# Attention over all keys by pairs of heads, with the row sums of the weights taken on GpSimd

## The chip, the cores and the metric

The kernel runs on one core of one Trainium2 chip. The metric is the device time of one execution in microseconds (us), the median of several runs. The engines are named as in the profile: PE (TensorE, matmuls), PEld (its weight loads), DVE (VectorE), ACT (ScalarE), POOL (GpSimd), SP (SyncE, which only issues DMAs).

## The reference

Two transformer blocks follow each other on 1024 tokens of width 1024, in float32. The change lies in the first block's attention: 8 query heads of width 64, heads 0 to 3 on one key and value head, heads 4 to 7 on the other, every query sees every key.

```
    def one_block(q_blk):
        s = jnp.einsum('bkgqd,bksd->bkgqs', q_blk, kt).astype(jnp.float32) * scale
        p = jax.nn.softmax(s, axis=-1).astype(vt.dtype)
        return jnp.einsum('bkgqs,bksd->bkgqd', p, vt)
```

Around it stand an input projection (23 tiles of 128 columns), a bidirectional mLSTM with 4 heads, an output projection and a gated feed-forward part. The second block has its own projections, an attention with forget gates and one over a sliding window.

## The kernel before

The kernel is written by hand for one core. A planner (`Plan`) first writes one list of steps; each engine then walks through the list and issues its own instructions for the steps that concern it, in that order, and semaphores hold the engines together. So the list sets the order on every engine, and an instruction that waits holds up all that stands behind it on its engine.

The full attention goes by jobs (kind, head h, half n of the queries: 512 columns), 16 in all, one after the other, h outermost. A job has 8 units, one for each 128 keys. All is kept transposed: keys on partitions, queries along the free dimension. For a unit:

- `sc`: PE makes 128x512 scores in one of two PSUM banks (2 and 3) with two matmuls, `qq,kk` and `qa,ka`; the second adds the low parts and, by a row of ones, minus the row maximum. ACT then takes the exponential into one of three buffers `full_pf`.
- `val`: PE multiplies these weights by the values. The stationary tile `full_v` is 128 keys x 128 columns: 64 columns of values and 64 of ones, so rows 64 to 127 of the result are the row sums. Both operands are float32; the profile shows each such product as two records. Banks 6 and 7 alternate by job.
- `max`: for a later job, PE makes scores once more with queries on partitions, and DVE takes the maximum of each row (8 of these per job, one per unit); `mrow` turns the 4x128 maxima into a row, which ACT writes into `full_qa`. `max`, `mrow` and some steps of the mLSTM's gates alternate between two further banks, 4 and 5.
- `take` and `div`: ACT turns the row sums into their inverse (Ln, then Exp with scale -1), DVE multiplies the 64x512 result by it.
- `qhi`, `qlo`: ACT and DVE split the queries of a later job into high and low parts, three buffers.

In `attention`, the step `sc` of the next unit stands ahead of `val` of this one. Between them `other(...)` takes portions of the input projection from a list (`fill`: nine matmuls each, L1218 to L1220), as long as there are any, and hooks place steps of the mLSTM there: its gates ("gate") beside units 3 to 63, the preparation of its first head beside the last 26 units. After the last job the first mLSTM outputs (L1456) wait until all 16 divisions are done.

Lines to follow: L1309 (`max` on PE), L1325 (`mrow` on PE), L1344 and L1346 (`sc`), L1368 (`val`), L1831 (exponential), L1839 and L1841 (`take`), L1811 (`mrow` on ACT), L2292 (maximum on DVE), L2156 and L2160 (DVE products and low parts).

## Time and profile before

| | us |
|---|---|
| median of 3 runs | 1990.89 |
| lowest and highest | 1988.49, 1994.8 |
| the profiled execution, device time | 1993.19 |
| its span in the trace | 1991.4 |
| the full attention's stretch of the trace | 279 to 520 |

How to read it: the span runs from the first to the last instruction; the device time of the same execution is 1.8 us more. Time in the trace is counted from the start of the span. Busy time of PE is summed over records that overlap, since a matmul's record runs from its start until its last result is written, while the next one has already begun; the distance from start to start, or the chain of work, tells what a matmul costs.

### The profile page before, as it was taken

The page shows a single profiled execution, that of the slowest core. Times are in us where ns is not written, and L with a number is a line of the kernel's source. Part 1 is how long each engine was busy: PE and PEld are TensorE (multiplying, and loading weights), DVE is VectorE, ACT ScalarE, POOL GpSimd, SP SyncE. Part 2 cuts the span into 40 slices and gives each one's busy share as a digit, 9 for nine tenths or more (in the row PEclk, how much of TensorE's full clock was granted, in tenths as well). Part 3 has the DMA queues.
Part 4 walks back from the last instruction along what each step waited for, and adds up shares of the span by engine and source line. Part 5 has one row for each costly group of instructions (what it writes and reads, how often), then busy time and mean ns, then how long its engine had stood idle before and what let it go on. Part 6 is the DMA issues. An engine that isn't in the chain of part 4 may idle for free.

```text
span 1991.4 us, 23686 instructions
## 1 busy us (share of the span) xinstructions
PE 1929.0 (97%) x8844; PEld 1507.2 (76%) x8844; DVE 1209.3 (61%) x1774; ACT 909.6 (46%) x1523; POOL 104.3 (5%) x188
## 2 busy tenths in 40 slices
PE   6999999999999989999999999999999999999898
PEld 4778876656787768888888788887888887776577
DVE  7795847655576787677555546656453555345744
ACT  6543345565553542332333434434523665455652
POOL 1101100000000000111000100000011000000000
PEclk9999999999999999999999999999999999999999
DMA  8426510010204423345111653333432000114052
GB/s 329 158 96 212 189 33 11 1 53 1 96 1 164 164 96 122 142 180 201 69 70 53 216 207 122 112 128 137 163 132 74 33 32 33 31 39 165 1 180 95
DMA packets 67151, 216.13 MB, mean 109 GB/s; under 512 B 8272, under 2 KB 13520, under 8 KB 66784
## 3 DMA queue, kind: packets, MB, share of 16 engines
q1 hardware_dynamic: 47168, 141.15, 20.1%
q0 software_dynamic: 19872, 73.48, 10.2%
q8 instruction: 72, 1.18, 0.2%
q14 instruction: 39, 0.32, 0.0%
HBM read 177.30 MB, written 34.61 MB: 106 GB/s over the span
## 4 chain that ended last, share of the span: by engine, by line
PE 85%; DVE 7%; ACT 3%; DMA 3%; issue 2%; SPq 0%; DVEq 0%; ACTq 0%
PE ps L1218 13%; PE ps L1220 13%; PE ps L1219 13%; PE ps L1368 9%; PE ps L1524 6%; PE ps L1525 6%; PE ps L1526 6%; PE ps L1344 3%; PE ps L1346 3%; DMA w_raw<-in_weights 2%; PE ps L1309 1%; DVE w_lo L2160 1%; PE ps L1312 1%; ACT w_hi L1691 1%; DMA ada_first<-in_ada 1%
## 5 line engine op out<-in xcount | busy, mean ns | idle before, releaser
L1218 PE MATMUL ps<-h_hi,w_hi 128*128 128x512 f32 x832 | 334.7, 402 | 9.7 <-DVE h_lo L2160 6.5
L1220 PE MATMUL ps<-h_hi,w_lo 128*128 128x512 f32 x832 | 325.9, 392 | 0.0
L1219 PE MATMUL ps<-h_lo,w_hi 128*128 128x512 f32 x832 | 325.4, 391 | 0.0
L2160 DVE TENSOR_TENSOR w_lo<-w_raw,w_hi 128x1024 fp32r<-128x1024 f32 x139 | 170.0, 1224 | 237.3 <-ACT w_hi L1691 235.7
L1691 ACT ACTIVATE w_hi<-w_raw 128x1024 fp32r<-128x1024 f32 x140 | 147.7, 1056 | 239.0 <-DMA w_raw<-in_weights 238.8
L2292 DVE TENSOR_REDUCE mh<-ps 128x1 f32<-128x512 f32 (+1 forms) x224 | 140.2, 630 | 143.9 <-PE ps L1309 67.9
L1218 PEld LDWEIGHTS ps<-h_hi,w_hi 128*128 128x128 f32 x832 | 157.9, 190 | 45.1 <-DVE h_lo L2160 7.7
L1220 PEld LDWEIGHTS ps<-h_hi,w_lo 128*128 128x128 f32 x832 | 156.9, 189 | 34.0
L1219 PEld LDWEIGHTS ps<-h_lo,w_hi 128*128 128x128 f32 x832 | 157.4, 189 | 32.1 <-issue 1.4
L1218 PE MATMUL ps<-hid_hi,w_hi 128*128 128x512 f32 x352 | 138.1, 392 | 3.9 <-DVE hid_kept_lo L2160 2.1
L1524 PE MATMUL ps<-t_hi,pair_S_r 128*128 128x512 f32 x352 | 137.2, 390 | 4.4 <-DVE pair_S_r L2160 2.6
L1220 PE MATMUL ps<-hid_hi,w_lo 128*128 128x512 f32 x352 | 137.0, 389 | 0.0
L1525 PE MATMUL ps<-t_lo,pair_S_r 128*128 128x512 f32 x352 | 137.0, 389 | 0.0
L1526 PE MATMUL ps<-t_hi,pair_S_r 128*128 128x512 f32 x352 | 136.9, 389 | 0.0
L1368 PE MATMUL ps<-full_pf,full_v 128*128 128x512 f32 x256 | 131.0, 593 | 0.3 <-ACT full_pf L1831 0.2
L1831 ACT ACTIVATE second_pf<-ps 128x512 f32<-128x512 f32 (+2 forms) x128 | 65.1, 510 | 139.9 <-PE ps L1350 61.3
L1831 ACT ACTIVATE full_pf<-ps 128x512 f32<-128x512 f32 x128 | 76.2, 597 | 97.9 <-PE ps L1346 97.4
L1368 PE MATMUL ps<-second_pf,second_v 128*128 128x128 f32 (+3 forms) x336 | 113.4, 439 | 0.8 <-ACT second_pf L1831 0.7
L1344 PE MATMUL ps<-full_qq,full_kk 128*128 128x512 f32 x128 | 90.2, 705 | 0.2 <-issue 0.2
L1344 PE MATMUL ps<-second_qq,second_kk 128*128 128x128 f32 (+3 forms) x168 | 84.3, 502 | 1.7 <-ACT second_pf L1831 0.7
L1218 PEld LDWEIGHTS ps<-hid_hi,w_hi 128*128 128x128 f32 x352 | 66.1, 188 | 20.3 <-DVE hid_kept_lo L2160 2.9
L1524 PEld LDWEIGHTS ps<-t_hi,pair_S_r 128*128 128x128 f32 x352 | 66.1, 188 | 19.3 <-issue 4.0
(405 smaller groups left out, 3842.0 us busy)
## 6 DMA issues: line engine op xcount, KB each, us to landing
w_raw<-in_weights SPq DMA_DIRECT2D x140, 512.0 KB, 3.5
ada_next<-in_ada POOLq DMA_DIRECT2D x32, 512.0 KB, 4.7
ada_last<-in_ada POOLq DMA_DIRECT2D x24, 512.0 KB, 5.1
pair_gate<-in_weights SPq DMA_DIRECT2D x22, 512.0 KB, 3.5
pair_up<-in_weights SPq DMA_DIRECT2D x22, 512.0 KB, 4.5
ada_first<-in_ada SPq DMA_DIRECT2D x8, 1024.0 KB, 17.7
m_scratch<-y POOLq DMA_DIRECT2D x12, 512.0 KB, 5.9
hid_scratch<-hid_out POOLq DMA_DIRECT2D x22, 256.0 KB, 2.3
```

The source lines that it names most:

```text
L1218: e.matmul(o, w_hi[slot][:, tile_of(kw)], hi, start=start, stop=False, skip_group_check=skip)
L1219: e.matmul(o, w_hi[slot][:, tile_of(kw)], lo, start=False, stop=False, skip_group_check=skip)
L1220: return e.matmul(o, w_lo[slot][:, tile_of(kw)], hi, start=False, stop=stop, skip_group_check=skip)
L1344: e.matmul(o, A.kk[kb][:, keys], A.qq[b][:, q], start=True, stop=False, skip_group_check=True)
L1368: x = e.matmul(o, A.v[kb][:, kt, :], A.pf[p3][:, c:c + q1 - q0], start=(u == 0 and kind != "band"), stop=False, skip_group_check=True)
L1524: e.matmul(ps[:, bank, :], a_hi[:, tile_of(k)], b_hi[:, first + k, :], start=start and k == 0, stop=False, skip_group_check=True)
L1525: e.matmul(ps[:, bank, :], a_hi[:, tile_of(k)], b_lo[:, first + k, :], start=False, stop=False, skip_group_check=True)
L1526: x = e.matmul(ps[:, bank, :], a_lo[:, tile_of(k)], b_hi[:, first + k, :], start=False, stop=k == 3, skip_group_check=True)
L1691: return e.activation(dst, src, ACT.Copy)
L1831: e.activation(A.pf[p3][:, c0:c1], ps[:, bank, c0:c1], ACT.Exp, scale=SC).then_inc(s["p_exp"], 1)
L2160: return e.tensor_tensor(dst, src, hi.bitcast(F32), ALU.subtract)
L2292: x = e.tensor_reduce(A.mh[b][:, half, i:i + 1], ps[:, bank, 0:k1 - k0], AX_X, ALU.max)
```

## The change

The order of the full attention's work and the form of its value product are changed; the second block's attention is not.

- Jobs are paired: heads 2m and 2m+1 with the same n. Units of the two alternate (`paired` takes the place of `attention` for this part).
- The value product has only the 64 columns of values as its stationary tile (64 instead of 128 columns). The even head writes PSUM rows 0 to 63 of a bank, the odd head rows 64 to 127 of the same bank. In the built program the two have tiles of 128x64 at column 0 and at column 64 of the array; all other large matmuls have 128x128. Products are issued in groups of four (V_GROUP), which alternate between the two halves.
- The row sums come from elsewhere: GpSimd adds the weights of the 8 units of each head (`psum`, 7 additions of 128x512 per job, 112 in all), and two matmuls per pair against 64 columns of ones (`dsum`) sum them over partitions into the auxiliary banks.
- `take` and `div` are done once for each pair on 128 partitions: 8 instead of 16.
- There are six weight buffers instead of three, four query buffers instead of three.
- All 16 maxima of a pair stand beside units 1 to 12 of the pair before it; the last four units of each pair have none.
- GpSimd's queue also gets one instruction that reloads its library ahead of the first addition.
- Some semaphores are merged; the columns of ones are no longer written into `full_v`.

```diff
+V_GROUP = 4
+def paired(p, jobs, fill, share, at):
...
+    for m, start in enumerate(starts):
+        a, b = jobs[2 * m], jobs[2 * m + 1]
+        steps = [("max", *job, u) for job in (a, b) for u in max_units_of(*job)]
+        low, high = (starts[m - 1] + 1, start - 4) if m else (-4 - len(steps), -4)
+        at_g = [low + n * (high - low + 1) // len(steps) for n in range(len(steps))]
+        for g, step in zip(at_g, steps):
+            maxima.setdefault(g, []).append(step)
+        rows.setdefault(at_g[len(steps) // 2 - 1] + 2, []).append(("mrow", *a))
+        rows.setdefault(start - 2, []).append(("mrow", *b))
...
+    for g, (i, u) in enumerate(units):
...
+        if g + 1 < len(units):
+            p.add("sc", *jobs[units[g + 1][0]], units[g + 1][1])
+        for step in rows.get(g, []) + waiting + queries.get(g, []) + maxima.get(g, []):
+            p.add(*step)
+        waiting = [("div", *x[1:]) for x in waiting if x[0] == "take"]
+        if u:
+            p.add("psum", *job, u)
+        if g and g % V_GROUP == 0:
+            products(units[g - V_GROUP:g])
+        if i % 2 and g == last[i]:
+            ended.append((g + 3, job))
+        if ended and ended[0][0] == g:
+            p.add("dsum", *ended[0][1])
+            waiting.append(("take", *ended.pop(0)[1]))
+        other(share(job))
...
-                self.v = [v_area[i](f"{n}_v{i}", [P, KT, P], F32) for i in range(2)]
+                self.v = [v_area[i](f"{n}_v{i}", [P, KT, 64 if n == "full" else P], F32) for i in range(2)]
...
+                if kind == "full":
+                    e.matmul(ps[rows_of(h), bank, :], A.v[kb][:, u, :], weights[:, :], start=u == 0, stop=u == KT - 1,
+                             skip_group_check=True).then_inc(s["val"], 1)
+                    return
...
+            def weight_sums(kind, h, n):
+                bank, sums = aux_bank("dsum", kind, h, n), A1.sums[take_no(kind, h, n) % 2]
+                aux_free(("dsum", kind, h, n))
+                e.wait_ge(s["p_sum"], no("psum", kind, h, n, KT - 1))
+                for odd in range(2):
+                    x = e.matmul(ps[rows_of(odd), bank, :], ones[:, 0:64], sums[odd][:, :], start=True, stop=True, skip_group_check=True)
+                x.then_inc(s["den_mm"], 1)
...
-                if i > 3:
-                    e.wait_ge(s["val"], i - 3)
+                if i > back:
+                    e.wait_ge(s["val"], i - back)
+                    if kind == "full":
+                        e.wait_ge(s["p_sum"], summed(i - back))
...
+                if kind == "full":
+                    e.wait_ge(s["val"], no("val", kind, h, n, KT - 1))
+                    tt(y[:, QA + h // 2, half_of(n)], ps[:, 6 + job % 2, :], A1.rinv[0][:, :], ALU.mult).then_inc(s["div"], 1)
+                    return
...
+            def weight_sum(kind, h, n, u):
+                pair, i = take_no(kind, h, n), no("sc", kind, h, n, u)
+                total = A1.sums[pair % 2][h % 2][:, :]
+                e.wait_ge(s["p_exp"], i)
+                if u == 1:
+                    if pair >= 2:
+                        e.wait_ge(s["den_mm"], pair - 1)
+                else:
+                    e.wait_ge(s["p_sum"], no("psum", kind, h, n, u - 1))
+                e.tensor_tensor(total, weights_at(kind, i - 2)[:, :] if u == 1 else total, weights_at(kind, i)[:, :], ALU.add).then_inc(s["p_sum"], 1)
```

PE's order in the middle of the full attention, past the input projection, before the change (names: `full_qq2` is the query buffer, `full_kk1` the second key head, `full_pf0` to `full_pf2` the weight buffers):

```order
L1344 MATMUL ps<-full_qq2_141,full_kk1_136 128x512
L1346 MATMUL ps<-full_qa2_144,full_ka1_138 128x512
L1309 MATMUL ps<-full_kk1_136,full_qq0_139 128x512
L1368 MATMUL ps<-full_pf1_148,full_v1_146 128x512
L1344 MATMUL ps<-full_qq2_141,full_kk1_136 128x512
L1346 MATMUL ps<-full_qa2_144,full_ka1_138 128x512
L1309 MATMUL ps<-full_kk1_136,full_qq0_139 128x512
L1368 MATMUL ps<-full_pf2_149,full_v1_146 128x512
```

The same place after the change, around the border of two pairs (L1462 and L1464 are `sc`, L1427 is `max`, L1443 `mrow`, L1485 `val`, L1499 `dsum`):

```order
L1443 MATMUL ps<-ident_r_84,mx1_1_154 1x128 x4
L1462 MATMUL ps<-full_qq0_139,full_kk1_136 128x512
L1464 MATMUL ps<-full_qa0_142,full_ka1_138 128x512
L1462 MATMUL ps<-full_qq1_140,full_kk1_136 128x512
L1464 MATMUL ps<-full_qa1_143,full_ka1_138 128x512
L1485 MATMUL ps<-full_pf0_147,full_v0_145 64x512
L1485 MATMUL ps<-full_pf1_148,full_v0_145 64x512
L1485 MATMUL ps<-full_pf2_149,full_v0_145 64x512
L1485 MATMUL ps<-full_pf3_150,full_v0_145 64x512
```

And the rows a few places further down, with the sums of the pair that has ended:

```order
L1427 MATMUL ps<-full_kk1_136,full_qq2_141 128x512
L1499 MATMUL ps<-p_sums10_166,ones_81 64x512
L1499 MATMUL ps<-p_sums11_167,ones_81 64x512
L1462 MATMUL ps<-full_qq0_139,full_kk1_136 128x512
L1464 MATMUL ps<-full_qa0_142,full_ka1_138 128x512
L1427 MATMUL ps<-full_kk1_136,full_qq2_141 128x512
```

One value product stood between any two units' scores; now four stand together, and between the groups scores of four units follow each other. Even and odd weight buffers belong to the even and the odd head.

At the end of the attention PE had, before:

```order
L1368 MATMUL ps<-full_pf0_147,full_v1_146 128x512
L1368 MATMUL ps<-full_pf1_148,full_v1_146 128x512
L1407 MATMUL ps<-ident_80,y_124 128x128 x8
L1456 MATMUL ps<-m_v0_207,m_w0_198 128x129 x2
```

and has now (L1537 and L1586 are the former L1407 and L1456):

```order
L1485 MATMUL ps<-full_pf4_151,full_v1_146 64x512
L1485 MATMUL ps<-full_pf5_152,full_v1_146 64x512
L1485 MATMUL ps<-full_pf0_147,full_v1_146 64x512
L1485 MATMUL ps<-full_pf1_148,full_v1_146 64x512
L1499 MATMUL ps<-p_sums10_166,ones_81 64x512
L1499 MATMUL ps<-p_sums11_167,ones_81 64x512
L1537 MATMUL ps<-ident_80,y_124 128x128 x8
L1586 MATMUL ps<-m_v0_207,m_w0_198 128x129 x2
```

The last two matmuls of `dsum` stand ahead of the transposes L1537 and wait for GpSimd's last addition.

## Rows read from the trace of the kernel before

**Rows 1.** The page: engines over the whole span.

```profile
PE 1929.0 (97%) x8844; PEld 1507.2 (76%) x8844; DVE 1209.3 (61%) x1774; ACT 909.6 (46%) x1523; POOL 104.3 (5%) x188
```

**Rows 2.** Busy time by stretch: us, then each engine's busy us (instructions), clock, DMA.

```profile
279.00:520.00 241.00, 237.91 (x901) 147.31 (x900) 143.37 (x227) 131.80 (x227) 0.00 (x0) 1.00 0.04 14
```

**Rows 3.** Waits from 279 to 520: us in total, times, longest.

```profile
ACT full_pf L1831 <- PE ps L1346: 97.4, 99, 3.0
DVE mh L2292 <- PE ps L1309: 63.7, 66, 3.1
...
PEld ps L1344 <- ACT full_pf L1831: 8.1, 14, 0.8
```

**Rows 4.** The chain of work, 366.4 to 371: start, us, what.

```profile
368.44 0.23 PE ps L1220
368.67 0.86 PE ps L1368 x2
369.53 0.23 PE ps L1344
369.76 0.23 PE ps L1346
370.00 0.23 PE ps L1309
```

**Rows 5.** Instruction groups, 275 to 521: busy us, mean ns; idle before.

```profile
L1368 PE MATMUL ps<-full_pf,full_v 128*128 128x512 f32 x256 | 131.0, 593 | 0.3 <-ACT full_pf L1831 0.2
...
L1346 PE MATMUL ps<-full_qa,full_ka 65*128 65x512 f32 x128 | 50.7, 396 | 0.0
L1309 PE MATMUL ps<-full_kk,full_qq 128*128 128x512 f32 x120 | 48.4, 403 | 0.0
L1220 PE MATMUL ps<-h_hi,w_lo 128*128 128x512 f32 x30 | 11.8, 393 | 0.0
...
L1325 PE MATMUL ps<-ident_r,mx 128*1 128x128 f32 x64 | 6.5, 223 | 3.6 <-issue 2.4 <-DVE mh L2292 1.0
...
L1831 ACT ACTIVATE full_pf<-ps 128x512 f32<-128x512 f32 x128 | 76.2, 597 | 97.9 <-PE ps L1346 97.4
L1841 ACT ACTIVATE rinv<-rinv 64x512 f32<-64x512 f32 x16 | 10.1, 631 | 0.5
L1839 ACT ACTIVATE rinv<-ps 64x512 f32<-64x512 f32 x16 | 9.5, 593 | 1.6 <-PE ps L1368 1.2
L1811 ACT ACTIVATE full_qa<-ps 1x512 fp32r<-1x512 f32 x16 | 9.3, 584 | 5.7 <-PE ps L1325 5.4
L1691 ACT ACTIVATE full_qq<-y 64x512 fp32r<-64x512 f32 x13 | 8.1, 622 | 0.2
...
L2292 DVE TENSOR_REDUCE mh<-ps 128x1 f32<-128x512 f32 x120 | 82.2, 687 | 66.3 <-PE ps L1309 65.7
```

**Rows 6.** PE's instructions in order of time around one `mrow`: start, us.

```profile
353.94 0.39 PE L1346 MATMUL ps<-full_qa,full_ka 65*128 65x512 f32 x1
354.46 0.40 PE L1325 MATMUL ps<-ident_r,mx 128*1 128x128 f32 x4
354.70 0.47 PE L1309 MATMUL ps<-full_kk,full_qq 128*128 128x512 f32 x1
355.02 0.39 PE L1218 MATMUL ps<-h_hi,w_hi 128*128 128x512 f32 x1
```

**Rows 7.** GpSimd's compute groups over the whole span.

```profile
L2745 POOL CAST band_low<-cmask 128x128 bf16<-128x128 f32 x2 | 2.0, 1016 | 0.0
...
L2753 POOL MEMSET second_v<- 128x512 f32 x2 | 1.1, 531 | 0.1
...
L3107 POOL MEMSET const-float32-1.0<- 128x1 f32 x1 | 0.1, 103 | 0.0
```

**Rows 8.** All engines in order of time at the attention's end.

```profile
518.55 0.60 ACT L1831 ACTIVATE full_pf<-ps 128x512 f32<-128x512 f32 x1 [0.73 <-PE ps L1346]
...
522.39 0.38 PE L1456 MATMUL ps<-m_v,m_w 128*128 128x129 f32 x1 [1.19 <-DVE y L2156]
```

More of the change, by code:

```diff
@@ L832, in build @@
         area = Area(156.25, 174)
[L833 to L837 removed]
+        A1 = Buffers("full", four(64, 72, 80, 88), four(68, 136), area, (76, 92, 144, 94, 146, 78))
+        A1.mx = [area(f"mx1_{i}", [P, 4], F32R) for i in range(4)]
+        A1.mh = [area(f"mh1_{i}", [P, 2, 4], F32) for i in range(4)]
+        area = Area(112, 116)
+        A1.qq.append(area("full_qq3", [P, HT], F32R))
+        A1.qa.append(area("full_qa3", [P, HT], F32R))
+        A1.rinv = [Area(148, 150)("rinv1", [P, HT], F32)] * 2
+        A1.sums = [[Area(start, start + 2)(f"p_sums{i}{odd}", [P, HT], F32) for odd, start in enumerate(starts)]
+                   for i, starts in enumerate(((138, 150), (116, 118)))]
         A2 = Buffers("second", four(104, 108, 112, 116), four(132, 136), Area(120, 132), (148, 152, 156))
@@ L1029, in build @@
         G_COLS = {12: 1, 13: 2, 14: 3, 18: 4}
-        AUX = [x for x in plan.steps if x[0] in ("vprep", "max", "mrow") or x[0] == "gate" and x[1] in G_COLS]
+        AUX = [x for x in plan.steps if x[0] in ("vprep", "max", "mrow", "dsum") or x[0] == "gate" and x[1] in G_COLS]
         AUX_NO = {x: i for i, x in enumerate(AUX)}
@@ L1445, in m_outputs @@
                 if i == 0:
-                    e.wait_ge(s["div"], 16)
+                    e.wait_ge(s["div"], FULL_TAKES)
                 elif d:
@@ L2914, in back @@
                 e.wait_ge(s["val"], no("val", "full", last, 1, KT - 1))
+                if part:
+                    e.wait_ge(s["p_sum"], no("psum", "full", last, 1, KT - 1))
                 e.wait_ge(s["m_kept"], 16 * len(KEPT_ORDER))
```

208 lines of the change are left out of this document (139 added, 69 removed).

## The prediction

> **What bounds the kernel now.** I read the page first: PE is busy 97% of the span, the next engine, DVE, 61% [rows 1]. Then the busy time by stretch: in the full attention, 279 to 520, PE has 237.9 of 241 us, ACT 131.8, DVE 143.4 and GpSimd nothing, at full clock [rows 2]. Then the waits: the large ones are those of ACT and DVE for PE (97.4 and 63.7 us); PE's own wait for an exponential is 8.1 us [rows 3]. So PE is the bound and the others have slack. The change touches this stretch only: from the first memory outputs on, PE's order is the old one. What counts is PE's issue time in these 241 us, and how much of ACT's and DVE's slack it eats.
>
> The chain of work gives prices from start to start: 0.23 us for one matmul of 512 columns, 0.86 for a value product in its two records, so 0.43 a record [rows 4]. With the counts of the groups [rows 5]: 256 score matmuls x 0.23 = 58.9; 120 maxima x 0.23 = 27.6; 128 value products x 0.86 = 110.1; 88 matmuls of the input projection x 0.23 = 20.2; the 16 `mrow` of four short matmuls some 5; the gates and the preparation of the memory some 13 (my estimate from the number of their instructions). That is 235; the remaining 6 are PE's waits today.
>
> **The value products (removed 110, added 69).** The 64 new columns do not shorten a product by themselves: `mrow` loads one column and still pays for its moving columns (four of 128 in 0.24 us, against 0.23 for one of 512) [rows 6]. A gain comes only if products of the two halves of the array run at once. No row of this trace shows two tiles side by side, so I bound it: nothing overlaps (0.86 each), or all does (0.43 for each of the two, half). I take a value between, from the order: the two records of one product use the same half and follow each other, so at strictly ordered starts only the second record of one product can run with the first record of the next, in the other half. Four alternating products are then 5 steps of 0.43 = 2.15 us instead of 3.44. 32 groups x 1.29 = 41.3 us less. The full overlap would be 4 steps, 1.72 us, 55.0 less.
>
> The Trainium skill (TensorE: Matmul & The Clock Gate, Part 3) says that three column tiles measured 2.38 times as fast. Spread evenly this is an efficiency of 0.79 a tile, an estimate of 1.59 for two, and 3.44 / 1.59 = 2.17 us; its twofold bound gives the 1.72. No run here shows it yet.
>
> **The sums on PE (added).** Two products per pair against ones: 3 steps of 0.43 = 1.29, x 8 = 10.3 us (6.9 with full overlap, 13.8 with none).
>
> **Change of tile width (added).** 32 groups and 8 sums, 40 visits to the narrow tiles. `mrow` is such a visit today: its four matmuls start 354.46, the next at 354.70, but the one after at 355.02, 0.32 instead of 0.23 later [rows 4, 6]. 0.09 a visit, 3.6 us.
>
> **Sum of PE's issue time: -41.3 + 10.3 + 3.6 = -27.4 us.** (-44.5 with full overlap.)
>
> **Stalls that come back.** Before, the value product between two scores gave ACT 1.55 us for an exponential of 0.60 [rows 4, 5]. Now four units of scores stand together. With two banks, the scores i+2 start when exponential i has ended; they need 0.63 until written (0.23 + 0.40) and some 0.1 for two signals, the exponential 0.60: 1.35 us for two units, 0.675 each. PE's work is 0.46 a unit, 0.69 with one maximum. So units with a maximum just fit, and units without wait.
> - The last four units of each pair have no maxima: 4 x 0.675 = 2.7 of ACT's pace, and one `mrow` (0.58) and one `qhi` (0.62) stand in ACT's queue there, 3.9 us, against 1.84 of scores and 0.3 of `mrow` on PE: 1.8 us of waiting.
> - Behind `dsum` PE has more maxima, and the second needs the bank that ACT's Ln empties. On ACT the Ln stands behind an exponential whose scores come after `dsum`: Ln ends some 1.86 us behind `dsum`, PE is there after 1.15: 0.7 us. Whoever waits is PE, with scores and products queued behind.
> - DVE in the first four units of a pair has six maxima (4.1 us [rows 5]), a low part, a copy and a division, some 5.9, against 4.5 + 2.15 on PE: it fits behind the products.
>
> 2.5 us x 8 pairs = 20, less the 6 that today's stretch already has: +14. Eight portions of the projection (2.05 us each) still give ACT time in the early pairs, the gates' long operations on ACT and DVE take it back; I let them cancel.
>
> **GpSimd (added, off the path).** 112 additions of 128x512. Nothing like it is in the trace. The same shape written without reading takes 0.53 us, 0.10 of it fixed; a cast of 128x128 takes 1.02, four times that is 4.06 [rows 7]. If a read costs what the write costs (0.43), an addition takes 0.96 to 1.4; I take 1.2. A pair then costs GpSimd 14 x 1.2 = 16.8 us. It has some 28.7 (the stretch that I forecast, 229.6, by 8), and 24 where no projection is left (16 x 0.46 + 16 x 0.23 + 4 x 2.15 + 1.29 + 0.7 for `mrow` and visits = 21.6, and 2.5 of stalls). Six buffers let it lag by some three units. The cover is gone at 1.7 us an addition in the late pairs, at 2.05 in all. The fixed cost of its library comes while it is idle.
>
> The Trainium skill (GPSIMD Engine Reference, 3.1) has 4497 ns for an addition of 2048 float32, an estimate of 1.12 us for 512; by it this work stays hidden.
>
> **ACT, DVE, copies.** 8 pairs of Ln and Exp less (0.59 + 0.63 [rows 5]), 8 divisions less, `full_v` without ones: all on engines that wait for PE, worth nothing by themselves. The additional buffers add no instruction.
>
> **The end.** Before, from the last exponential's start (518.55) to the first memory output it is 3.84 us [rows 8]: product, Ln, Exp, division. Now four products (2.15 instead of 0.86) and `dsum` (1.29) stand there, and the last additions end some 2.7 us behind the exponential, so they are no later than the products. About 2 us more.
>
> **Sum.** -27.4 + 14 + 2 = -11.4 us. The profiled execution took 1993.2 (span 1991.4 and 1.8 around it), which gives 1981.8; it lies 2.3 above the median of the runs, so 1979.5, and I say 1979.
>
> **Rivals.**
> 1. Full overlap of the halves, the second record of one head with that of the other: -44.5 + 14 + 2 = -28.5, 1962. For it: nothing in the rows forbids it. Against it: the order of starts. It is also where ACT would bind sooner, so 1962 is near the best. Chance 0.14.
> 2. The overlap is there, but waits eat it: each narrow visit drains PE, and the four units in a row run at ACT's pace everywhere. A drain is a record's 0.39 less the 0.23 = 0.16 us on the way in and again on the way out, 40 x 0.32 = 12.8 instead of 3.6: +9, 1988. For it: the large matmuls' records overlap today by just this, and the visit of `mrow` is to a single column. Against it: that visit shows 0.09. Chance 0.17.
> 3. The change doesn't do what its form says: no overlap of float32 products in the two halves. Then 0 saved, 13.8 for the sums, 3.6 for the visits, 14 of stalls (fewer, perhaps 8, since PE is slower), 2 for the end: +27 to +33, 2018 to 2024. It ends on the other side. It decides as soon as four products take more than 2.5 us (11.4 / 32 = 0.36 above the 2.15). Against it: the program does give the two products separate column tiles. For it: each is two records with two weight loads, and no row shows tiles at once. Chance 0.15.
> 4. GpSimd becomes the bound: at 2.4 us an addition a pair takes 33.6 us, 8 pairs 269 against 229.6, so 2018; it decides from 2.15 us on (0.1 x 112 = 11.4 above the 2.05). At the upper bound of 4.06 it would be 455 us, 2205. For it: the one measured operation that reads is the slow cast. Against it: the cast converts, the addition does not. Chance 0.07.
>
> The Trainium skill (TensorEngine Tiling (Array Packing), Key Properties) says that changing the tiling mode drains TensorE; this would be the second rival's time.
>
> **Numbers.** The forecast itself has 0.47, its own range 1968 to 1987. A measurement of this kernel tells some 0.3% from no change, 6 us, so faster means below 1985. The forecast and the first rival give 0.61 less a small tail, plus a little of the second: 0.61 faster. The second rival and that tail: 0.14 same. The rest, 0.25, is slower. For 8 in 10 the range starts at 1962 (the first rival) and ends at 2014, a little below the third rival's 2018 to 2024 and the fourth's, which with GpSimd's upper bound are the 2 in 10 left out.
>
> **What the profile after would show.** The chain of work should have some 2.2 us for a group of four products, starts of odd and even ones closer than 0.86 and partly at once; L1499 1.3 us a pair. ACT's waits for scores should fall from 97 us to some 60, and PE should wait for L1967 in the last units of a pair, some 1 to 2 us. GpSimd's addition should read 1.0 to 1.4 us, with waits of PE for it near zero. The attention's stretch should shrink from 241 to some 230 us, and nothing else should change. I am wrong if a group takes 2.5 us or more, if an addition takes 2.1 or more, or if PE's new waits for ACT pass 3.9 us a pair (2.5 and 11.4 / 8).

## The result, and the profile after

The changed kernel takes 2023.46 us (median of 4 runs, 2022.32 to 2025.12), the kernel before 1991.26 beside it: 1.0157 times as long, 95% interval 1.0144 to 1.0169. It is slower, and outside the range forecast. The profiled execution's span is 2021.5 us against 1991.4.

The page of the changed kernel, busy time of each engine and the chain that ended last:

```profile
PE 1921.4 (95%) x8876; PEld 1477.6 (73%) x8876; DVE 1227.7 (61%) x1766; ACT 894.1 (44%) x1507; POOL 260.4 (13%) x300
...
PE 74%; issue 9%; DVE 7%; POOL 4%; ACT 3%; DMA 2%; SPq 0%; DVEq 0%; POOLq 0%; ACTq 0%
```

PE had 97% [rows 1]. The second line has POOL with 4% of the chain, an engine that the forecast put off the path. This share says less than it seems: the chain is followed back from its end, it enters GpSimd's queue where PE waits 1.52 us for the last additions, and from there it runs back through that queue; the 9% of `issue` lie beside it. Busy time by stretch in the full attention (columns: the stretch, its length, PE, PEld, DVE, ACT and POOL busy, the granted clock, DMA share, GB/s):

```profile
279.00:300.00 21.00, 18.07 (x80) 12.08 (x80) 12.42 (x20) 10.97 (x17) 4.51 (x4) 1.00 0.08 26
300.00:330.00 30.00, 25.89 (x106) 14.15 (x104) 23.19 (x26) 16.56 (x27) 21.08 (x15) 0.98 0.05 18
330.00:360.00 30.00, 25.25 (x86) 12.67 (x88) 19.89 (x20) 9.40 (x16) 16.55 (x11) 0.79 0.00 0
360.00:400.00 40.00, 30.27 (x112) 15.30 (x108) 27.05 (x31) 11.87 (x22) 20.89 (x14) 0.91 0.00 1
400.00:440.00 40.00, 35.60 (x148) 16.40 (x148) 23.08 (x35) 20.24 (x38) 24.19 (x19) 0.96 0.13 46
440.00:480.00 40.00, 35.12 (x133) 15.96 (x129) 23.07 (x35) 18.91 (x32) 25.03 (x19) 0.91 0.05 22
480.00:520.00 40.00, 36.44 (x155) 19.45 (x154) 25.43 (x42) 15.73 (x28) 22.68 (x18) 0.87 0.00 0
520.00:552.00 32.00, 29.39 (x152) 15.57 (x150) 8.53 (x17) 16.74 (x39) 20.27 (x17) 1.00 0.02 4
```

Before, PE was busy in 238 of 241 us at a clock of 1.00 [rows 2]. Now it stands still for 3 to 10 us in each stretch, and from 330 on the clock is at 0.79 to 0.96 in five of them: a mixture of the levels 2.4 GHz (1.00) and 1.2 GHz (0.50).

From the first score to the end of the last value product, and PE's share of it, in one row:

```profile
288.00:549.00 261.00, 226.23 (x913) 114.69 (x911) 157.50 (x211) 116.95 (x210) 154.32 (x112) 0.92 0.03 13
```

Before, the same piece of work was 279 to 520. So the 30 us are 9 of a later start, 19 of a longer attention and 2 to 3 at its end; behind it the kernel is the old one.

What PE, ACT and DVE waited for between 270 and 560 (us in total, times, longest):

```profile
ACT full_pf L1967 <- PE ps L1464: 106.5, 65, 8.1
DVE mh L2434 <- PE ps L1427: 72.6, 39, 5.7
...
PEld ps L1427 <- DVE mh L2434: 24.2, 30, 4.3
PEld ps L1443 <- DVE mh L2434: 12.9, 6, 4.2
...
PE ps L1427 <- DVE mh L2434: 11.7, 9, 4.0
PE ps L1443 <- DVE mh L2434: 9.9, 5, 3.8
...
PEld ps L1462 <- ACT full_pf L1967: 8.4, 16, 1.3
PEld ps L1485 <- ACT full_pf L1967: 7.7, 24, 0.5
...
ACT full_pf L1967 <- POOL p_sums L2988: 3.3, 3, 1.9
...
PE ps L1462 <- ACT full_pf L1967: 1.2, 2, 1.0
```

The new rows are the four with DVE's `mh`: PE waits for DVE's maxima, L1427 because a maximum needs a bank that DVE has emptied, L1443 because the row is made of the maxima. PE's waits and PEld's are largely the same stalls seen twice, so they aren't added. The wait for ACT, which the forecast looked for, has grown a little. The scores' weight loads wait 8.4 us for exponentials, as they did (8.1 in [rows 3]), and those of the products 7.7 us, where they had waited 2.5; PE itself stands 1.2 us for it.

The value products themselves did better than forecast. PE in order of time, at the full clock (start, us, line, count):

```profile
306.02 1.94 PE L1485 MATMUL ps<-full_pf,full_v 128*64 128x512 f32 x8
307.89 0.50 PE L1462 MATMUL ps<-full_qq,full_kk 128*128 128x512 f32 x1
308.22 0.40 PE L1464 MATMUL ps<-full_qa,full_ka 65*128 65x512 f32 x1
...
365.77 1.08 PE L1499 MATMUL ps<-p_sums,ones 128*64 128x512 f32 x4
366.78 0.50 PE L1462 MATMUL ps<-full_qq,full_kk 128*128 128x512 f32 x1
```

Eight records, four products, and the next score starts 1.87 us later. A pair's sums, two products, take 1.01. So two products more cost 0.86, which is 0.43 for each, half of the 0.86 of before: the overlap is full. What is left in both, 0.15, is the price of going to the narrow tile and back.

And this is where time goes, all engines around 325 us:

```profile
325.53 2.65 DVE L2465 TENSOR_TENSOR_SCAN g_f_log<-g_f_log,g_zeros 32x1024 f32<-32x1024 f32 x1
...
326.71 4.21 POOL L2988 TENSOR_TENSOR p_sums<-p_sums,full_pf 128x512 f32<-128x512 f32 x2 [0.67 <-ACT full_pf L1967]
...
328.21 1.57 DVE L2302 TENSOR_TENSOR full_qa<-y,full_qq 64x512 fp32r<-64x512 f32 x1
329.71 0.68 DVE L2434 TENSOR_REDUCE mh<-ps 128x1 f32<-128x512 f32 x1
330.42 0.69 DVE L2298 TENSOR_TENSOR y<-ps,rinv 128x512 f32<-128x512 f32 x1
...
330.45 0.79 PE L1427 MATMUL ps<-full_kk,full_qq 128*128 128x512 f32 x1 [2.77 <-DVE mh L2434]
```

The maximum that PE waits for is read by DVE at 329.71, behind a scan of the gates and a low part, which take 2.65 and 1.57 us while GpSimd adds (2.28 and 0.68 before, in the mean); PE stands for 2.77. The next group of four products, PE alone in order of time:

```profile
331.17 3.68 PE L1485 MATMUL ps<-full_pf,full_v 128*64 128x512 f32 x8
```

That is nearly twice 1.94: from 331.2 to 334.7 the granted clock is 0.50, the lower level, right behind the wait. Of the 32 groups seven take 3.2 to 3.6 us to the next score, each behind a stall of 1.2 to 4.0 us, and 23 take 1.87. DVE's groups in 285 to 552 (line, tiles, count, busy us, mean ns, idle before):

```profile
L2434 DVE TENSOR_REDUCE mh<-ps 128x1 f32<-128x512 f32 x112 | 74.1, 683 | 67.0 <-PE ps L1427 66.6
L2302 DVE TENSOR_TENSOR full_qa<-y,full_qq 64x512 fp32r<-64x512 f32 x13 | 14.6, 1121 | 9.3 <-ACT full_qq L1821 9.1
L2415 DVE CAST full_qq<-y 64x512 fp32r<-64x512 f32 x13 | 8.9, 688 | 4.2 <-PE ps L1464 3.9
L2298 DVE TENSOR_TENSOR mx<-mh 128x4 fp32r<-128x4 f32 x15 | 8.3, 554 | 0.5
L2465 DVE TENSOR_TENSOR_SCAN g_zeros<-g_i_pre 32x1024 f32<-32x1024 f32 x2 | 6.5, 3272 | 0.0
...
L2298 DVE TENSOR_TENSOR g_f_pre<-g_i_pre,g_zeros 32x1024 f32<-32x1024 f32 x2 | 4.4, 2176 | 0.0
```

and GpSimd's in 285 to 556:

```profile
L2988 POOL TENSOR_TENSOR p_sums<-p_sums,full_pf 128x512 f32<-128x512 f32 x96 | 134.2, 1417 | 79.7 <-ACT full_pf L1967 79.3
L2988 POOL TENSOR_TENSOR p_sums<-full_pf,full_pf 128x512 f32<-128x512 f32 x16 | 21.1, 1330 | 67.1 <-ACT full_pf L1967 67.1
```

The maxima, which read PSUM, take what they took (683 ns against 687). Those operations of DVE with two inputs in SBUF that run beside additions take up to 1.1 us more in the mean: this scan 2274 ns before, 3272 now, `g_f_pre` 1210 and 2176, the low part 683 and 1121, `mx` 161 and 554. Others hardly change (the scan of `g_f_log` 2280 and 2464), and one operation with a single input gets longer too: the cast of the queries, 422 and 688. An addition takes 1.25 us at its shortest and up to 3.27 at its longest.

### The profile page after: what moved, and what is told of

Its sections match the earlier page's. It is cut to its first block, busy times and chain, and to the rows that moved or that the text cites. A ratio compares the mean times of both kernels' runs of the same rounds, so it can differ in the third digit from the quotient of the medians.

```text
span 2021.5 us, 23948 instructions
## 1 busy us (share of the span) xinstructions
PE 1921.4 (95%) x8876; PEld 1477.6 (73%) x8876; DVE 1227.7 (61%) x1766; ACT 894.1 (44%) x1507; POOL 260.4 (13%) x300
## 3 DMA queue, kind: packets, MB, share of 16 engines
q1 hardware_dynamic: 47168, 141.15, 20.3%
## 4 chain that ended last, share of the span: by engine, by line
PE 74%; issue 9%; DVE 7%; POOL 4%; ACT 3%; DMA 2%; SPq 0%; DVEq 0%; POOLq 0%; ACTq 0%
PE ps L1336 13%; PE ps L1338 13%; PE ps L1337 13%; PE ps L1654 6%; PE ps L1656 6%; PE ps L1655 6%; PE ps L1490 4%; POOL p_sums L2988 4%; DMA w_raw<-in_weights 2%; PE ps L1462 1%; PE ps L1464 1%; DVE w_lo L2302 1%; PE ps L1430 1%; PE ps L1784 1%; PE ps L1783 1%
## 5 line engine op out<-in xcount | busy, mean ns | idle before, releaser
L2988 POOL TENSOR_TENSOR p_sums<-p_sums,full_pf 128x512 f32<-128x512 f32 x96 | 134.2, 1417 | 79.7 <-ACT full_pf L1967 79.3
L1462 PE MATMUL ps<-second_qq,second_kk 128*128 128x128 f32 (+3 forms) x168 | 83.5, 498 | 1.7 <-ACT second_pf L1967 0.7
L1336 PE MATMUL ps<-mix_hi,w_hi 128*128 128x512 f32 x192 | 75.9, 396 | 2.7 <-DVE y L2581 1.3
```

Of the source, the lines that this page charges most:

```text
L1336: e.matmul(o, w_hi[slot][:, tile_of(kw)], hi, start=start, stop=False, skip_group_check=skip)
L2988: e.tensor_tensor(total, weights_at(kind, i - 2)[:, :] if u == 1 else total, weights_at(kind, i)[:, :], ALU.add).then_inc(s["p_sum"], 1)
```

## The experiments

Before these runs my theory was: GpSimd's additions lengthen DVE's long operations, the maxima behind them come late, PE may run only two maxima ahead, stands, and its clock falls. Rivals: the form of the products costs more than it saves somewhere else; the maxima stand in the wrong places whoever adds; the clock falls for another reason than the waits. Kernel times are medians; ratios are against the kernel before on the same chip. The ratio is the better number where two calls are compared, since the kernel before itself had medians from 1991.1 to 1993.3.

**e1: no additions.** GpSimd's 112 additions are left out, with the waits for them; four memsets fill the sums once.

```diff
-                e.tensor_tensor(total, weights_at(kind, i - 2)[:, :] if u == 1 else total, weights_at(kind, i)[:, :], ALU.add).then_inc(s["p_sum"], 1)
+                if u == 1 and pair < 2:
+                    e.wait_ge(s["p_exp"], i)
+                    e.memset(total, 1.0).then_inc(s["p_sum"], 1)
```

> The changed kernel, but GpSimd's 112 additions are left out (the sums are buffers of ones, so the row sums are not those of the weights); all matmuls, maxima and their order stay. Theory A (the additions hold up DVE's operations with two inputs in SBUF, which stand between the maxima in DVE's queue; PE then stands still and its clock falls): the scans and two-input operations go back from 2.1 to 3.3 us to the 1.2 to 2.3 us of before, PE's waits for DVE shrink to less than half, the clock stays at 1.0, and the time falls from 2023 to 1990 or below. Theory B (the order alone does it: four score units in a row, 16 maxima beside 12 units, two auxiliary banks): DVE's operations shorten, but PE's waits stay, 2010 or more.

Measured: 2002.42 us, ratio 1.0049 (1.0032 to 1.0066): 21 us less than the changed kernel, and still slower than before. DVE's rows in 285 to 527 are back at their old sizes:

```profile
L2463 DVE TENSOR_TENSOR_SCAN g_zeros<-g_i_pre 32x1024 f32<-32x1024 f32 x2 | 4.5, 2274 | 0.0
...
L2296 DVE TENSOR_TENSOR mx<-mh 128x4 fp32r<-128x4 f32 x14 | 2.3, 163 | 0.5
```

The time lies between those of the two theories. At 326.7 PE stands 1.67 us for a maximum, at the place where the changed kernel stands 2.77, so of that stall 1.1 us is the additions'. From the first score to the end of the last value product it is 240.9 us instead of 260.7, and PE's waits there for maxima are 15.0 us instead of 21.3. (The first score is 2.6 us earlier here, but so is the first maximum, 264.0 instead of 266.6, and the first addition comes only at 294: that is no effect of the additions.) PE still waits for maxima, and its clock still falls behind such waits, as this piece of PE's timeline shows:

```profile
358.70 0.50 PE L1427 MATMUL ps<-full_kk,full_qq 128*128 128x512 f32 x1 [0.47 <-ACT rinv L1974]
360.33 0.52 PE L1427 MATMUL ps<-full_kk,full_qq 128*128 128x512 f32 x1 [1.13 <-DVE mh L2432]
360.78 3.57 PE L1485 MATMUL ps<-full_pf,full_v 128*64 128x512 f32 x8
```

So the additions are 21 us of it, and the order by itself costs as well.

**e2: both heads in the same half.** The odd head's products go to the columns and rows of the even one, so nothing can overlap.

```diff
-                    e.matmul(ps[rows_of(h), bank, :], A.v[kb][:, u, :], weights[:, :], start=u == 0, stop=u == KT - 1,
+                    e.matmul(ps[0:64, bank, :], A.v[kb][:, u, :], weights[:, :], start=u == 0 and h % 2 == 0, stop=u == KT - 1 and h % 2 == 1,
```

> The changed kernel, but the odd head's value product is written to the same 64 rows as the even head's, so both use the same half of the array (the two heads' values are added up, rows 64 to 127 are left as they were). Theory A (products of the two halves overlap fully, a group of four takes 1.9 us at 2.4 GHz): now a group takes 3.5 us at 2.4 GHz and the time rises by 20 to 50 us over 2023. The third rival of the prediction (no overlap at all, the group's 3.5 us in parts of the trace are its true price): the groups that take 1.9 us stay, and so does the time, within 5 us.

Measured: 2073.94 us (one run), 50.5 more than the changed kernel. The group of four that took 1.94:

```profile
310.07 3.65 PE L1485 MATMUL ps<-full_pf,full_v 128*64 128x512 f32 x8
```

The next score starts 3.58 us behind it instead of 1.87; 32 times the difference is 55, so the size fits too. The overlap comes from the two halves, and it is what the change lives on.

**e3: the gates' operations elsewhere.** Their steps on DVE and ACT go to the last units of the pairs, where no maxima stand.

```diff
-        unit(3 + 4 * part, ("gate", part))
-    for part, g in ((16, 82), (17, 86), (18, 90)):
+        unit(16 * (part // 3) + (13, 15, 16)[part % 3], ("gate", part))
+    for part, g in ((16, 95), (17, 96), (18, 98)):
```

> The changed kernel with the steps of the mLSTM's gates moved from every fourth unit to units 13, 15 and 16 of each pair, where no maxima wait (the last three to units 95, 96 and 98). The additions stay. Theory A: the long DVE operations still get longer under the additions but no maxima stand behind them, so most of PE's waits of 2 to 4 us go and the clock holds; 1985 to 2000. Theory B (bunched maxima alone): 2015 or more.

Measured: 2006.12 us, ratio 1.0079 (1.0054 to 1.0103), 17 less than the changed kernel, though not the 1985 to 2000 that I expected. The seven runs lie far apart (2003 to 2021), and the profiled one is the longest, so no row of it is used.

**e4: three edits.** The gates moved; `dsum` writes the bank of the next pair's values instead of an auxiliary one; and the maximum of two columns is a reduction, which takes one input, instead of an operation with two.

```diff
-                bank, sums = aux_bank("dsum", kind, h, n), A1.sums[take_no(kind, h, n) % 2]
-                aux_free(("dsum", kind, h, n))
+                pair = take_no(kind, h, n)
+                bank, sums = 6 + (pair + 1) % 2, A1.sums[pair % 2]
...
+                elif kind == "full":
+                    e.tensor_reduce(A.mx[b][:, :], A.mh[b][:, :, :].rearrange("p h q -> p q h"), AX_X, ALU.max).then_inc(s["mcol"], 1)
```

> The moved gates together with two further edits: the weight sums' two matmuls go to the value bank of the next pair instead of an auxiliary bank, and the maxima of the two halves are joined by a reduction of one input instead of a maximum of two. Theory A: each takes away one more wait (for ACT's Ln some 10 us on PE's side, for the joined maxima up to 0.4 us each of 16), 1970 to 1990, below the kernel before the change. Theory B: 2010 or more.

Measured: 2000.41 us, ratio 1.0039 (1.0022 to 1.0056), 6 us less than e3. The 1970 to 1990 that I expected was missed.

**e5: four banks as well.** From the end of the projection of this part to the first memory step, the maxima and the small matmuls take turns in four banks.

```diff
-            return 4 + AUX_NO[step] % 2
+                bank = (4, 5, 0, 1)[n4 % 4] if last_y1 < i < first_mk else 4 + n4 % 2
```

> The kernel of e4_three_edits (2000 us), and from unit 42 to unit 101, where the projection no longer uses banks 0 and 1, maxima and their rows go round four banks instead of two. Theory A2 (what is left is PE held at the maxima because DVE is up to three operations behind and two banks let PE run only two ahead): PE's waits for DVE in these 60 units nearly vanish and the time falls by 5 to 12 us, to 1988 to 1995. Theory B2 (what is left is ACT's pace, one exponential in 0.675 us against 0.46 us of scores, and the low clock): less than 3 us.

Measured: 1996.9 us, ratio 1.0021 (1.0011 to 1.003). The 3.5 us less than e4 are fewer than theory A2's 5 to 12, and the intervals of the two ratios overlap.

**e6: groups of two.** The gates moved, the reduction for `mx`, and:

```diff
-V_GROUP = 4
+V_GROUP = 2
```

> The kernel of e3_gates_moved with the joined maxima by a reduction, and value products in groups of two instead of four: 64 visits to the narrow tiles instead of 32. Theory A2: a visit costs 0.15 us more than the products themselves, so 5 us are added, and the finer mixture gives back about as much on DVE's side: 1998 to 2006. Theory B2 (four score units in a row at ACT's pace cost 1 to 2 us a pair and more): it falls below 1995.

Measured: 2006.36 us, ratio 1.0071 (1.0056 to 1.0086). A group of two takes 1.01 us to the next score, 0.86 and 0.15. Nothing is gained against e3's 2006.12. But the 32 visits more cost 32 x 0.15 = 4.8 us, so the finer mixture and the reduction together give back about as much, as theory A2 said. ACT's pace is not worth more than that.

**e7: e5 without additions.** The edits of e5 and of e1 together; the waits for the sums go as well:

```diff
-                    if kind == "full":
-                        e.wait_ge(s["p_sum"], summed(i - back))
```

> The kernel of e5_four_banks without GpSimd's additions (sums are buffers of ones, so the row sums are not those of the weights). If the loss is the additions' hold on DVE plus the held maxima, nothing is left of it: the value products' 44 us show but for some 20 us of ACT's pace, 1970 to 1978. If it stays above 1985, the pairwise order itself (the later start of the first unit, ACT's pace, the low clock) costs more than I think.

Measured: 1979.54 us, ratio 0.9932 (0.9916 to 0.9949). It is the only one well below the kernel before, and it leaves out work that the result needs. The 1970 to 1978 that I expected was missed by 1.5 us. The attention in one row:

```profile
288.00:508.00 220.00, 205.87 (x913) 113.30 (x913) 130.64 (x211) 117.23 (x210) 2.06 (x4) 0.99 0.04 15
```

Against the changed kernel's 261 us that is 41 less: PE stands for 14.1 us instead of 34.8, and for as many records of matmuls (913) it is busy 205.9 instead of 226.2, since the clock is 0.99 and not 0.92. So half of what was lost is waiting and half is the clock. (The profiled execution is the longest of this kernel's four, 1984.63 us; if anything the difference is larger.)

**e8: every maximum's matmul issued twice.** The changed kernel with 128 more matmuls of 0.23 us, 112 of them inside the attention: 26 us of work there.

```diff
+                        e.matmul(ps[:, bank, 0:k1 - k0], q(qt), A.kk[kb][:, k0:k1], start=True, stop=True, skip_group_check=True)
                         x = e.matmul(ps[:, bank, 0:k1 - k0], q(qt), A.kk[kb][:, k0:k1], start=True, stop=True, skip_group_check=True)
```

> The changed kernel with the matmul of each of the 128 maxima issued twice into the same bank (same result). It adds 128 x 0.23 = 29 us of work to PE. Theory C (the clock falls because PE has too little to do beside its waits, and the low clock costs some 20 us): the mean clock of the attention rises and the time grows by less than 15 us. Theory D (the clock does not answer to such work): it grows by 20 to 30 us and the clock stays near 0.9 in this stretch.

Measured: 2028.7 us (two runs), ratio 1.0181 (1.0161 to 1.0201): 5 us more than the changed kernel. Its attention:

```profile
288.00:552.00 264.00, 239.17 (x1024) 131.24 (x1022) 155.02 (x211) 116.90 (x210) 152.25 (x112) 0.97 0.04 13
```

26 us of work, and the attention is 3 us longer, as theory C has it. PE stands for 24.8 us instead of 34.8, so 10 us went into standing time; and its busy time rose by 13 only, since the clock is at 0.97 instead of 0.92. The other 13 us were given back by the clock, which is higher here, where PE is kept at work.

**e9: the additions on DVE.** As e5, with the 112 additions on DVE, a unit later; GpSimd does nothing here.

```diff
-        if u:
-            p.add("psum", *job, u)
+        if g and units[g - 1][1]:
+            p.add("psum", *jobs[units[g - 1][0]], units[g - 1][1])
...
-            work = {"psum": weight_sum, "yt": y_tile,
+            work = {"yt": y_tile,
```

> The edits of e5 (gates moved, sums' bank moved, maximum of two columns by a reduction, four banks for maxima), and all 112 additions on DVE, one unit later, instead of on GpSimd. Mine (the price of the additions is that GpSimd's reads and writes hold DVE's operations with two inputs in SBUF, not the additions' own time): an addition of 512 costs DVE some 0.6 us (estimate: the division of the same shape, 0.69, reads PSUM too), 112 make 67 us, on top of some 143 in a stretch of 225: DVE then is nearly full. If it still fits, scans read 2.27 us and two-input operations 1.2 again, and the time is between e7 (1979.5) and e5 (1996.9), some 1988. Rival (DVE's queue is what counts, whoever adds): 67 us more in DVE's order delay the maxima more than 112 x 1.28 us on GpSimd did, PE waits for DVE's maxima by 20 us or more over e5's 24, and the time is 2005 to 2030.

Measured: 2013.32 us, ratio 1.0099 (1.0078 to 1.0119): 16 more than e5. My expectation fell. An addition and the attention as a whole:

```profile
L2904 DVE TENSOR_TENSOR p_sums<-p_sums,full_pf 128x512 f32<-128x512 f32 x96 | 64.6, 681 | 1.9 <-ACT full_pf L1987 1.6
```

```profile
288.00:537.00 249.00, 218.17 (x916) 116.39 (x914) 195.50 (x323) 117.28 (x210) 0.00 (x0) 0.95 0.04 13
```

The additions take 0.68 us each, 76 in all, half of what they cost GpSimd, and the scans are back at 2.28 us; but DVE is busy 195.5 of 249 us, and its maxima are late although no operation is lengthened. The rival's time came out, its size of the waits did not: from the first score to the last value product PE stands 30.8 us against 23.0 in e5, 8 more and not 20, and another 7 are longer work at a clock of 0.95 instead of 0.98. So what counts is how long a maximum waits in DVE's order, whatever fills it.

**e10: half and half.** As e5, the even heads' additions on DVE, the odd heads' on GpSimd, the same function in both queues:

```diff
+                if h % 2:
+                    return
```

(DVE; on GpSimd `if not h % 2`.)

> As e5, but the additions of the even heads on DVE and those of the odd heads on GpSimd, each with a semaphore of its own. Mine: half of GpSimd's load and so about half of what it takes from DVE's two-input operations, some 8 us of the 17 between e5 and e7, while DVE takes 56 x 0.6 = 34 us in a stretch with some 80 us to spare: 1988 to 1994, so at or a little below the kernel before. Rival (DVE's queue counts): above e5's 1996.9, some 2000 to 2010.

Measured: 2011.34 us, ratio 1.0099 (1.0084 to 1.0114). The rival's side again, 1 us above its range: the half that DVE takes over costs 14 us more than it gives back. DVE's additions read 0.94 us here instead of 0.68, and GpSimd's 1.36, so the two sets also hold each other up.

**e11: four banks alone**, the diff of e5 on the changed kernel.

> The changed kernel with nothing edited but four banks for the maxima and the small matmuls instead of two (units from the last input projection on). Theory A (PE waits because it may run only two maxima ahead of DVE): the waits of L1427 and L1443 for DVE's maxima, 57 us by the changed kernel's lists of waits, fall to 30 or less, its granted clock stays at 1.00 in more of the stretches, and the time is 2005 to 2012. Theory B (DVE's order is late as a whole, the banks only put off the wait): 2018 or more; the step from e4 to e5, 3.5 us, would then be all that banks give.

Measured: 2012.23 us, ratio 1.0101 (1.0081 to 1.0121), 11 us less than the changed kernel. That is at the upper edge of theory A's time, but its other signs did not come. PEld's waits at L1427 (12.7 us in 285 to 552, against 21.3) fall by less than half, those at the rows hardly (11.5 against 12.9), where more banks can't help, and the clock of the attention is 0.92, as in the changed kernel; the profiled execution is the longest of the four. So the banks are worth 11 us, by a way that the rows show only in part. After the other edits they gave only 3.5 (e4 to e5): the edits don't add up.

**e12: portions of the projection earlier.** As e5, one behind every second of the first pair's maxima.

```diff
-        other(0.3)
+        other(0.5)
```

> The edits of e5, and of the input projection's portions one behind every second of the first pair's 16 maxima instead of one behind every third or fourth, so more of them stand ahead of the attention and fewer inside it; their sum is the same. Mine (of the 9 us by which the first scores start later, some 5 to 6 are waits of PE for DVE's maxima, which two banks let it run only two ahead of): maxima in twos need no such wait but for the first, 268.9 in the changed kernel's trace, so some 2 to 4 us of PE's waits go, and the time is 1993 to 1995. Rival (the portions inside the attention are what gives ACT and DVE their time there, and keeps PE's waits down): what is won at the start is lost between 300 and 360, where fewer portions stand between the scores; the time is 1997 or more.

Measured: 1990.29 us (11 runs), ratio 0.9995 (0.9986 to 1.0004), 6.6 less than e5 (5 by the ratios), even with the kernel before and better than the 1993 to 1995 that I expected. 33 matmuls of the projection, 7.6 us of work, have moved ahead of the first score. From the first maximum to the first score it takes 24.9 us instead of 22.8, so they cost 2.1 there: PE stands 1.5 us in this piece instead of 4.1, and the clock is 1.00 instead of 0.93. Inside the attention their work had been paid in full, 226.6 us against 234.0.

**e13: the rows a unit later.** As e12.

```diff
-        low, high = (starts[m - 1] + 1, start - 4) if m else (-4 - len(steps), -4)
+        low, high = (starts[m - 1] + 1, start - 5) if m else (-5 - len(steps), -5)
...
-        rows.setdefault(at_g[len(steps) // 2 - 1] + 2, []).append(("mrow", *a))
+        rows.setdefault(at_g[len(steps) // 2 - 1] + 3, []).append(("mrow", *a))
```

> The edits of e12, and each head's row of maxima is built on PE one unit further behind its last maximum. Mine (what is left between e12 and the kernel without additions is mostly PE waiting at the two rows of a pair for DVE's last maxima, which the additions make late: 7.2 us on PE at L1456 in e12's list of waits, with 10.0 on PEld at the same places): a unit more, 0.7 to 1 us, covers most waits of 0.93, the waits of L1456 fall below 3 us, and the time is 1984 to 1988, 0.2 to 0.4% faster than the kernel before. Rival (the wait moves with the row: DVE is late as a whole, since it has one maximum more to do by then, and ACT has a unit less to make the query from the row): the time is 1989 to 1992, as e12.

Measured: 1989.94 us (11 runs), ratio 0.9989 (0.9976 to 1.0002). The rival's time. PE's waits at the row itself for DVE did not fall below 3 us but rose from 7.2 to 10.0, PEld's at the same line from 10.0 to 13.2, and those of L1440 on PE from 1.6 to 3.9: DVE is late as a whole, and the wait goes with the row.

**e14: all portions first.** As e12, with:

```diff
-        other(0.5)
+        other(1)
```

> The edits of e12, but a whole portion of the input projection behind each of the first pair's maxima, so nearly all portions stand ahead of the first scores. Mine (PE has always work between two maxima at the start, and the portions inside the attention give PE nothing where it waits, since they stand at fixed places): the waits of PE for DVE's maxima before the first scores end, 1 to 3 us less, 1988. Rival (portions between the scores are the time in which ACT and DVE catch up): PE waits more for ACT's exponentials and DVE's maxima in the first three pairs, whose scores have then nothing between them, and its clock falls there: 1993 or more.

Measured: 1995.03 us (11 runs), ratio 1.0009 (0.9996 to 1.0022). The rival's time, 5 us above e12 by the medians and 3 by the ratios, whose intervals overlap a little. In 300 to 330 the clock is 0.89 (1.00 in e12) and PE busy 24.2 us (27.9). This speaks for some portions between the scores, though fewer than the change leaves there.

## Why the prediction was wrong

- **The value products: right in kind, too small.** Forecast 2.15 us for four, with full overlap (1.72) as a rival at 0.14. Measured 1.87 with the visit in it, 1.72 and 0.15. Before, four took 3.44 [rows 4], so 32 x 1.57 = 50 us less, where 41.3 less 2.9 for 32 visits of 0.09 was forecast. The argument from strictly ordered starts failed: in the trace the first records of an even and an odd product start together (306.02 and 306.03), then both second records (306.50 and 306.51), so eight records go in four steps. The sums are 8 x 1.01 = 8 us with their visits instead of 11. Together -42, where the forecast was -27.4, some 15 us better. A visit costs 0.15, not the 0.32 of the second rival. The first rival, full overlap, had a chance of 0.14 and was right on this term.
- By the Trainium skill (TensorE: Matmul & The Clock Gate, Part 3), three column tiles run 2.38 times as fast. For two tiles 3.44 / 1.87 = 1.84 was measured, better than the 1.59 that I spread from it.
- **The step that failed: "it fits behind the products", and "I let them cancel".** DVE was added up a pair at a time with operations of the size that the trace of before shows, and compared with the length of four units. Both halves of that were wrong. Additions make DVE's operations longer, those with two inputs in SBUF and the cast, by 26 us over the attention (157.5 us busy for 211 instructions, against 131.3 for as many in e1). And what matters is not whether DVE's sum fits: the gates' scans stand between two maxima in a queue that PE may outrun by two banks only, so a long one can become a stall of PE (the 2.77 us that end at 330.45). Moving the gates away gives 17 us back (e3). The forecast for waits was +14 net, with 6 us of waits before; PE stood still for only 3.1 of them [rows 2]. A kernel with the additions left out and the places mended (e7) has about 24 us back from the 42 saved: from the first score to the last value product's end it was 241.4 before (278.9 to 520.3), less 3.2 for moved work and 42.1 is 196.1, and e7 takes 220.5, 10 more than the 14 forecast. That they are of one size is in part luck: in e7 PE stands 14.1 us, 7.9 of them for DVE's maxima, which the forecast had at nothing, and 2.6 for ACT. The changed kernel takes 260.7, so it has 65 back.
- By the Trainium skill (SBUF — State Buffer, Who interferes with whom), a DVE instruction with two inputs in SBUF contends with a GpSimd instruction that reads SBUF, and a reduction doesn't. The trace agrees in both: a scan goes from 2274 to 3272 ns, the maxima read 687 and 683. The page gives no duration for it. That rule spoke against this change, and the prediction didn't weigh it.
- **"GpSimd (added, off the path)": the size right, the place wrong.** Forecast 1.2 us an addition, measured 1.25 at the shortest and 1.4 in the mean, 155 us in all, and PE waits 1.5 us for it once. By its own count it was hidden but for the end. It costs 21 us all the same (e1), 17 with everything else mended (e5 to e7), nearly all of it through another engine's operations: its own length shows in 3.3 us of waits of ACT for a weight buffer and in 1.7 us at the end. The fourth rival looked at GpSimd's length alone.
- **The clock wasn't in the forecast.** Every wait was priced at its own length. In the attention the clock falls to 0.92 in the mean; e7 and the changed kernel differ by 20.7 us of standing and by 20.3 of longer work. The changed kernel and e1 differ by 10.0 of standing and 9.8 of longer work, e5 and e7 by 8.9 and 4.6. So a wait here costs one and a half times to twice itself. e8 is the test: 29 us more of matmuls, 5 us more of time, and a higher clock (0.97 instead of 0.92).
- **The start, left out.** 9 us: some 3.2 is moved work (6 more maxima, the second head's row and 6 matmuls of the projection now stand ahead of the first score), 3.0 is PE standing for DVE's maxima and rows (4.1 us from the first maximum to the first score, against 1.0). 1.2 lies ahead of the first maximum, where nothing was changed; this point lies between 263.8 and 266.6 in the profiles of all these kernels, so it is scatter. For the other 1.6 no row was found.
- **The end: near in size, wrong in the reason.** Forecast some 2 us more; from the last value product's end to the first memory output it is 4.7 us instead of 2.1. The forecast had the last additions end no later than the products. They end 1.4 us behind them, and PE waits for them:

```profile
546.23 1.09 ACT L1967 ACTIVATE full_pf<-ps 128x512 f32<-128x512 f32 x2 [1.93 <-POOL p_sums L2988]
...
546.58 1.94 PE L1485 MATMUL ps<-full_pf,full_v 128*64 128x512 f32 x8
...
550.04 1.08 PE L1499 MATMUL ps<-p_sums,ones 128*64 128x512 f32 x4 [1.52 <-POOL p_sums L2988]
```

  In e1 this piece is 2.9 us, so 1.7 of it is GpSimd's own length.
- **ACT's pace (second rival, and the last four units).** Not what binds in the changed kernel: PE stands 1.2 us for exponentials, its weight loads 16.1 us (10.6 before), and e6 with groups of two comes out even with e3.

Sum of it, from the forecast's -11: the products and sums 15 better; 9 for the start; 40 more of waiting and clock inside the attention than e7 has (260.7 - 220.5), and e7's 24 are 10 more than the 14 forecast; less the 3.2 of work that has moved out. That is -11 - 15 + 9 + 40 + 10 - 3 = +30, and the spans differ by 30.1. The sum must come out, since its large terms are differences of the traces; what is shown beyond it is that 21 us of it go with the additions.

Still open: what share of the 40 us each place has by itself. The edits overlap (four banks 11 alone, 3.5 behind the others), so only their sum is shown. No run gives DVE its old durations with the additions still on GpSimd: that their 21 us come through DVE rests on DVE's rows, on the stall that ends at 330.45 (1.67 us without them) and on the small direct waits for GpSimd. That the clock falls because PE stands is supported by e8 and by the seven slow groups, each behind a stall; no run held the waits and changed the clock alone, and not every stall is followed by a fall. Not tried is a form whose additions cost neither engine, for instance sums made by PE for some of the units.

## What to carry to other kernels

Two float32 products in the two column halves of the array cost one, and going there and back 0.15 us: the form is worth 42 us here at the full clock, before the waits that it brings. But an engine that is "off the path" is so only if it leaves the engines on the path their durations: before giving GpSimd work that reads SBUF, list which DVE operations with two SBUF inputs run beside it and what stands behind them in DVE's queue. And where PE is the bound at full clock, count each new stall for more than itself (up to twice here), and check the queue between two results that PE waits for, not the sum over a section.

## What the runs showed of the hardware

- Float32 products of 128x64 tiles in alternating halves overlap in full, though each is two records with two weight loads: 1.87 us to the next score for four, 1.01 for two (e6), 3.58 for four when both heads go to the same half.
- Stalls of PE of 1.2 to 4.0 us are often followed by work at the lower clock: groups of four read 1.94 us at one place and 3.68 at another (clock 0.50), and 3.57 in e1 behind waits of 0.47 and 1.13 us. Not always: the group at 373.3 in e1 stands right behind a stall of 2.91 us and takes 1.87 to the next score, at 1.00.
- GpSimd and DVE hold each other up: an addition of 128x512 takes 1.25 to 3.27 us, a scan of 32x1024 2.27 us alone and 3.27 beside additions, an operation on four columns 0.16 and 0.55, a cast of 64x512 0.42 and 0.69, all in the mean; maxima read from PSUM keep their 0.69. The same addition is 0.68 us on DVE alone, and 0.94 beside GpSimd's.
